# A chunked recurrence on a core of Trainium2: its small products spread over four 64x64 tiles of the matmul array, and a reordered stage ahead of it

## What is computed

```python
def wkv7_scan(r, decay, k, v, kk_neg, kk_b, reverse):
    def step(state, inp):
        r_t, w_t, k_t, v_t, an_t, b_t = inp
        sa = jnp.einsum('bhij,bhj->bhi', state, an_t)
        state = (state * w_t[:, :, None, :] + sa[..., None] * b_t[:, :, None, :]
                 + v_t[..., None] * k_t[:, :, None, :])
        return state, jnp.einsum('bhij,bhj->bhi', state, r_t)
...
rwkv_feat = centred_shift(proj[..., :RWKV_COLS], shift_taps)
...
for direction, reverse in ((0, False), (1, True)):
    ...
    y = y + wkv7_scan(heads(r), heads(decay), heads(k_dir), heads(v), -kk, kk * heads(a), reverse)
```

## Time and profile before

| | us |
|---|---|
| median of 3 runs (5455.51 to 5463.51) | 5456.74 |
| the profiled execution, whole | 5460.31 |
| its span, first to last instruction | 5458.5 |
| `rwkv_inputs` | about 1385 to 2060 of the span |
| `recurrence` | 2062 to 3275 |
| TensorE busy, of the span | 4692.6 (86%) |

### The profile page before, as it was taken

The page is one execution under the profiler, slowest core; times in us unless marked ns, Lnnn a source line. Parts: engine busy times, 40 slices in busy tenths (PEclk is TensorE's granted clock), DMA queues, the critical chain, the costliest instruction groups (busy, mean ns, idle before and its releaser), DMA issues. The chain is left out here.

```text
span 5458.5 us, 141686 instructions
## 1 busy us (share of the span) xinstructions
PE 4692.6 (86%) x60038; PEld 4316.4 (79%) x60038; DVE 3104.5 (57%) x6054; ACT 2090.0 (38%) x4040; POOL 1089.2 (20%) x829
## 2 busy tenths in 40 slices
PE   6878888886788877999999997881299999999998
PEld 5757666664677776999999995661199999999998
DVE  6867777775677774444444444556644444444443
ACT  3347777774455551111111111220044343434343
POOL 4432222221233332000000212210010101010100
PEclk9989999998899998999999998995599999999999
DMA  7810000000433322212122114430155555555553
GB/s 156 155 45 15 14 12 16 12 12 25 153 124 124 123 100 93 61 50 62 50 62 61 50 53 148 148 129 5 41 168 159 170 159 170 166 164 167 163 160 111
DMA packets 496709, 526.44 MB, mean 96 GB/s; under 512 B 74224, under 2 KB 434672, under 8 KB 496240
## 3 DMA queue, kind: packets, MB, share of 16 engines
q1 hardware_dynamic: 390256, 413.95, 23.8%
q10 hardware_dynamic: 92480, 62.93, 5.0%
q0 software_dynamic: 13504, 42.30, 3.5%
HBM read 372.12 MB, written 146.99 MB: 95 GB/s over the span
## 5 line engine op out<-in xcount | busy, mean ns | idle before, releaser
L2185 DVE TENSOR_TENSOR g_wlo<-g_raw,g_whi 128x2048 fp32r<-128x2048 f32 x192 | 439.1, 2287 | 129.6 <-ACT g_whi L2147 129.6
L615 PE MATMUL sapS<-KT,saq 128*128 128x512 f32 x1024 | 369.3, 443 | 123.0 <-ACT saprob L515 115.1
L2147 ACT ACTIVATE g_whi<-g_raw 128x2048 fp32r<-128x2048 f32 x192 | 365.8, 1905 | 246.3 <-DMA g_raw<-expert_w_gate 246.3
L568 DVE TENSOR_REDUCE samx<-sapS 128x1 f32<-128x512 f32 x512 | 352.5, 689 | 184.1 <-PE sapS L615 178.6
L2252 PE MATMUL g_pD<-g_whi,g_hh 128*128 128x256 f32 (+1 forms) x1536 | 437.4, 285 | 0.6
L2252 PE MATMUL g_pD<-g_whi,g_hl 128*128 128x256 f32 (+1 forms) x1536 | 429.4, 280 | 0.0
L2252 PE MATMUL g_pD<-g_wlo,g_hh 128*128 128x256 f32 (+1 forms) x1536 | 429.3, 279 | 0.0
L1426 DVE TENSOR_TENSOR d_zy<-d_zy,d_pZ 128x128 f32<-128x128 f32 x720 | 178.0, 284 | 416.2 <-PE d_pZ L1465 416.0
L523 ACT ACTIVATE saph<-sapT 128x512 fp32r<-128x512 f32 x512 | 305.8, 598 | 225.6 <-PE sapT L630 219.2
L505 POOL TENSOR_SCALAR saprob<-saprob,sarden 128x2048 f32<-128x2048 f32 x128 | 254.8, 1990 | 654.5 <-DVE sarden L587 654.5
L1115 PE MATMUL c_pP<-c_xh,c_whi 128*128 128x258 f32 x1120 | 343.2, 306 | 43.1 <-DMA c_gup<-g_lora_up 27.8
(11 more groups left out here) (383 smaller groups left out, 13246.1 us busy)
## 6 DMA issues: line engine op xcount, KB each, us to landing
g_raw<-expert_w_gate SPq DMA_DIRECT2D x64, 1024.0 KB, 5.3
g_raw<-expert_w_up SPq DMA_DIRECT2D x64, 1024.0 KB, 5.4
g_raw<-expert_w_down SPq DMA_DIRECT2D x64, 1024.0 KB, 5.2
ops<-c_ops SPq DMA_DIRECT2D x40, 1024.0 KB, 4.0
d_bd<-ops SPq DMA_DIRECT2D x80, 512.0 KB, 4.2
c_xh<-xT_hi SPq DMA_DIRECT2D x10, 1032.0 KB, 6.3
c_xl<-xT_lo SPq DMA_DIRECT2D x10, 1032.0 KB, 8.6
x_in<-x SPq DMA_DIRECT2D x20, 512.0 KB, 7.9
```

What stands on the lines that cost most here:

```text
L568: ins = dve.tensor_reduce(mx[:, h % 2, k:k + 1], pS[k][:], AX.X, ALU.max)
L615: mm = pe.matmul(pS[k][:], q[:, h // GH, h % GH, :], KT[:, 2 * (h // GH) + p, key0 + k * 512:key0 + (k + 1) * 512], start=(p == 0), stop=( ...
L2147: act.activation(w_hi[:, Q % NBUF, :, :], raw[:, Q % NRAW, :, :], ACT.Copy).then_inc(s["g_hi"], 1)
L2185: dve.tensor_tensor(w_lo[:, Q % NBUF, :, :], raw[:, Q % NRAW, :, :], w_hi[:, Q % NBUF, :, :].bitcast(F32), ALU.subtract).then_inc(s["g_lo" ...
```

## The change

In **`recurrence`**:

- Some products are written across: head h's product goes to the other half of the partitions (`heads(True, ...)`), that is, to the array's two other tiles (rows 0 to 63 with columns 64 to 127, and the reverse). Crossed are `between`, Z, `through`, `solved` and a new product x4 (below). x1, x2, x3, Y, `values`, `turned`, `state` and `out` stay straight.
- In the code a crossed and a straight product alternate, pair of heads by pair of heads: x1 with `through`, x3 with x4, the first half of x2 with `solved`, its second half with level 0's P, Z with Y. From level 1 on P is issued with the first calls of the block that it shares (`state`, `values`, `out`, `turned`); the rest of the block follows, straight alone. The order of the blocks changes: `values` is now before `turned`.
- x4 is added (16 calls a turn): d_zy's second half is computed by its own product into pZ, and no longer masked from d_br. Y goes to the upper half of pP's bank, since pZ now holds Z or x4. Semaphores d_Z and d_Y take the place of d_ZY.
- DVE's `begin` finishes direction 0 (d_br, then d_zy) before direction 1. The state update of direction 0 stands between the two masks of level 1, that of direction 1 after level 1's sums. ACT's copies follow the new order.

In **`rwkv_inputs`**: DVE does both `decays` at the start of a slot and moves `shift(n, 0)` ahead of the keys; ACT does `exps(q, 1)` ahead of `mid(n, 1)`; in even slots `bonus(q)` goes behind `tile(n, 5)` and `norms(n)` on TensorE.

```diff
@@ rwkv_inputs, ACT
                 mid(n, 0)
+                exps(q, 1)
                 mid(n, 1)
-                exps(q, 1)
@@ rwkv_inputs, DVE
                 decays(q, 0)
+                decays(q, 1)
+                shift(n, 0)
                 keys_b(q, 0)
                 keys_a(q, 0)
                 keys_c(q, 0)
-                shift(n, 0)
-                decays(q, 1)
+                if n % 2 == 0:
+                    shift(n, 1)
                 keys_b(q, 1)
-                shift(n, 1)
                 keys_a(q, 1)
                 keys_c(q, 1)
+                if n % 2:
+                    shift(n, 1)
@@ rwkv_inputs, PE
                     tile(n, 4)
-                    bonus(q)
                     tile(n, 5)
                     norms(n)
+                    bonus(q)
@@ recurrence, DVE
-                    dve.tensor_tensor(zy[par][g][:, :, 1, :], br[par][g][:, :, 0, :], bc(beside[:, 1 - g, 0:1, :], [P, RT, C]), ALU.mult).then_inc(s["d_in"], 1)
+                    dve.wait_ge(s["d_x4"], 2 * m + g + 1)
...
+                    dve.tensor_tensor(zy[par][g][:, :, 1, :], slim(pZ[g]), bc(beside[:, 1 - g, 0:1, :], [P, RT, C]), ALU.mult).then_inc(s["d_in"], 1)
...
                 for l in range(NL):
-                    between(n + 1, 1 - par, l)
+                    for g in range(2):
+                        between(n + 1, l, g)
+                        if l == 1 and g == 0:
+                            state(n, par, 0)
+                    for g in range(2):
+                        grown(n + 1, 1 - par, l, g)
                     if l == 1:
-                        state(n, par)
-                    grown(n + 1, 1 - par, l)
+                        state(n, par, 1)
@@ recurrence, PE
+            def heads(cross, out, l, r, first=True, last=True):
+                for h in range(2):
+                    mm = pe.matmul(out(halves[1 - h if cross else h]), l(halves[h]), r(halves[h]), start=first, stop=last)
+                return mm
...
+                for j in range(RT):
+                    mm = x1(par, g, j)
+                    if n is not None:
+                        through(1 - par, g, 2 * j)
+                        side = through(1 - par, g, 2 * j + 1)
...
+                can_x3(m, g)
+                for j in range(RT):
+                    mm = x3(par, g, j)
+                    side = x4(par, g, j)
...
+            def keys(m, par, g, n=None):
+                pe.wait_ge(s["d_br"], 2 * m + g + 1)
+                if n is not None:
+                    can_solve(n, g)
+                for j in range(RT // 2):
+                    x2(par, g, j)
+                    if n is not None:
+                        solved(1 - par, g, 2 * j)
+                        side = solved(1 - par, g, 2 * j + 1)
...
+                can_between(m, 0, g)
+                for j in range(RT // 2):
+                    mm = x2(par, g, RT // 2 + j)
+                    between(par, g, 0, 2 * j)
+                    side = between(par, g, 0, 2 * j + 1)
...
+            def grown(m, par, l, g):
+                pe.wait_ge(s["d_Pe"], 2 * (NL * m + l) + g + 1)
+                for j in range(RT):
+                    if l < NL - 1:
+                        side = grown_z(par, g, l, j)
+                    mm = grown_y(par, g, l, j)
...
+            def state_and_between(n, m, par, g):
+                pe.wait_ge(s["d_uc"], 2 * n + g + 1)
+                can_between(m, 1, g)
+                for j in range(RT):
+                    state(1 - par, g, j)
+                    side = between(par, g, 1, j)
+                side.then_inc(s["d_P"], 1)
+                for i in range(RT, 2 * RT):
+                    mm = state(1 - par, g, i)
+                mm.then_inc(s["d_sn"], 1)
```

More of the change, by code:

```diff
@@ L1335, in keys @@
                 for g in range(2):
[L1336 to L1339 removed]
+                    if more:
+                        values(n + 1, 1 - par, g)
                 for g in range(2):
[L1341 to L1342 removed]
@@ L1344, in values @@
-            def values(m, par):
+                    out(n, par, i, g)
                 for g in range(2):
[L1346 to L1370, removed]
+                    if more:
+                        turned(n + 1, 1 - par, g)
@@ L1371, in _ @@
+            for g in range(2):
+                keys(0, 0, g)
+            for g in range(2):
+                values(0, 0, g)
+            for g in range(2):
+                turned(0, 0, g)
             with act.Fori(0, NCH // 2 - 1) as i:
@@ L1452, in _ @@
             turn(NCH - 2, 0)
-            state(NCH - 1, 1)
+            for g in range(2):
+                state(NCH - 1, 1, g)
         @block.tensor
@@ L1458, in _ @@
             pe.wait_ge(s["d_dm"], 1)
-            def products(out, *terms):
-                for j in range(RT):
-                    for k, (l, r) in enumerate(terms):
-                        for h in halves:
-                            mm = pe.matmul(out(h, j), l(h, j), r(h, j), start=(k == 0), stop=(k == len(terms) - 1))
-                return mm
-            of = lambda m, x=None: (lambda h, j: m[h, j, :]) if x is None else (lambda h, j: m[h, j, x, :])
-            into = lambda m: lambda h, j: slim(m)[h, j, :]
@@ new lines, in turned_and_between, with between_alone @@
+            def turned_and_between(m, par, g):
+                pe.wait_ge(s["d_vc"], 2 * m + g + 1)
+                can_between(m, 4, g)
+                for j in range(RT):
+                    turned(par, g, j)
+                    side = between(par, g, 4, j)
+                side.then_inc(s["d_P"], 1)
+                for i in range(RT, 2 * RT):
+                    mm = turned(par, g, i)
+                mm.then_inc(s["d_bk"], 1)
+            def between_alone(m, par, l, g):
+                can_between(m, l, g)
+                for j in range(RT):
+                    mm = between(par, g, l, j)
+                mm.then_inc(s["d_P"], 1)
@@ L1517, in through @@
[L1517 to L1525 removed]
+                    grown(m, par, 1, g)
@@ L1562, in _ @@
-            begin(0, 0, 0)
-            keys(0, 0)
-            turned(0, 0)
-            values(0, 0)
-            for l in range(NL):
-                between(0, 0, l)
-                grown(0, 0, l)
-            for n in range(NCH - 1):
-                turn(n, n % 2, n // 2)
-            through(NCH - 1, 1)
-            solved(NCH - 1, 1)
-            state(NCH - 1, 1)
-            out(NCH - 1, 1)
+                    turned_and_between(m, par, g)
+                for g in range(2):
+                    grown(m, par, 4, g)
@@ L1577 @@
+            for g in range(2):
+                pe.wait_ge(s["d_tmp"], 2 * n + g + 1)
+                for i in range(3 * RT):
+                    mm = out(par, g, i)
+                mm.then_inc(s["d_yo"], 1)
 NE = 16
```

316 lines of the change are left out of this document (205 added, 111 removed).

## The result

The changed kernel takes **5403.8 us** (median of 4 runs, 5401 to 5417), the kernel before 5457.1; the ratio is 0.9905, with a 95% interval of 0.9887 to 0.9923. It is faster, as forecast, by 53 us and not by 443. The range on record, 4900 to 5305, doesn't hold it.

The account below looks back on a forecast made before the run. It took the recurrence to be bound by TensorE's two tiles, with stalls and a lower clock in `rwkv_inputs`. 5460.3 - 333 (recurrence) - 110 (`rwkv_inputs`) = 5017 us profiled, 5014 as median; range 4900 to 5305.

Parts of the forecast that it names:

- What bounds before: two tiles at 0.0295 us a record: Recurrence before: TensorE's 896 records a turn on two tiles, 0.0295 us each, in a turn of 29.55 us.
- Four tiles side by side: Recurrence: straight and crossed tiles work together though they share rows; four starts within 0.06 us in level 1.
- Rivals 1 and 2: Recurrence: starts limited as a whole (5301 us, 19%), or tiles that share rows disturb each other (6112 us, 6%).
- Rival 1: Recurrence: four tiles together get no more than 0.0295 us a record; 28.4 us a turn, 5301 us in all; 19%.
- "I take 0.4" for "issue": Recurrence, near the turn's end: added TensorE waits for instructions, 0.4 us a turn, between nothing and 1.2.
- The sum of 21.0 us: Recurrence: forecast length of a new turn, from 19.9 us over its levels plus additions of 0.7 and 0.4.
- The chain, 19.9 us: Recurrence: begin and levels 0 to 4 summed along TensorE's blocks and DVE's masks and sums, 19.9 us a turn.
- L1407 beside POOL's masking, 0.7 us: Recurrence: direction 1's L1407 slowed by coinciding with POOL's masking of d_kr, 0.7 us a turn, up to 0.95.
- Rival 3: Recurrence: the clock falls to its lower level, starts nearly twice as far apart; 33.1 us a turn, 5485 us; 3%.
- `rwkv_inputs`, 11.3 us a pair: Saving per pair of slots from shorter stalls, clock and earlier `c_wag`; 11.3 us, about 110 in all, bounds 38 and 133.
- `norms`: 2 less forecast: `rwkv_inputs`, odd slots: TensorE's 4.1 us wait at `norms` shrinks by 2 us; bounds 1.3 more and 4.1 less.
- The 1.5 for the earlier `c_wag`: `rwkv_inputs`, even slots: shifting `c_wag` earlier frees a bank earlier, saving 1.5 us a pair of slots.

Follow-up runs that it names:

- small_load: The changed kernel with operand loads from the third chunk on cut to two of 32 KB per direction, computing on old operands: 5350.3 us, ratio 0.9799.
- shift1: The changed kernel with `shift(n, 1)` put back ahead of `keys_b(q, 1)` in odd slots of `rwkv_inputs`: 5395.9 us, ratio 0.9879.
- bonus_only: The kernel before, with only `bonus` in even slots of `rwkv_inputs` issued after tile 5 and `norms`: 5408.5 us, ratio 0.9909.
- flip0: The changed kernel with products by the identity (`values`, `turned`) of the first row half written as one-pass transposes: 5589.0 us, ratio 1.0236.

## Why the prediction was wrong

- **What bounds before: two tiles at 0.0295 us a record.** Right, and what hid the other limit. 128 records of 32 or 64 columns, one page, take 128 x 0.0295 = 3.78 us on two tiles; a page is there after 3.81 (small_load). Both limits stood at nearly the same height, and only one could be seen. Before, a page came each 4.25 us, and the instruction queue stood in the profile; the prediction didn't read it.
- **Four tiles side by side.** Right: four starts within 0.02 us at the same place as forecast. Rivals 1 and 2 are wrong as mechanisms. Rival 1's size is nearly right (28.4 us a turn, measured 29.4): a limit on starts as a whole exists, as an average over pages, not between single starts.
- **"I take 0.4" for "issue".** This is the step that failed. The prediction saw 48.8 us of "issue", read it as an effect of the load, and bounded it at 1.2 us a turn by doubling it. 27.9 of the 48.8 are one wait at the stage's start, and the rest counts loads and matmuls; TensorE's matmuls had 0.25 us a turn. It is 6.5 now. A wait that is small since consumption is just slow enough doesn't double when consumption goes up by a third; it takes most of the gain. The sum of 21.0 us should have been held against 7.3 pages, 7.3 x 3.8 = 28 us.
- **The chain, 19.9 us.** Not tested fully. Turns of 25.2 us still follow the pages. 29.4 less 6.5 are 22.9 us, an upper bound; part of them is at the lower clock.
- **L1407 beside POOL's masking, 0.7 us.** Wrong, with little weight: its 68 records from 2113.6 to 3083.3 took 691 to 693 ns (it is L1412 now). VectorE busy 13 us a turn: right (524.39 / 40 = 13.1).
- **Clock.** Rival 3's sign came true (0.90 in the recurrence, 1.00 before), but not as the cause: the stall of 1.20 us at 2562.29 ends a stretch at 1.00, and 219 us of stalls are left at 0.95 in `small_load`. Its 33.1 us a turn did not come. In the windows above a page took 4.1 us at 0.58, almost without a stall, and 3.6 to 3.8 at 1.00 with one.
- **`rwkv_inputs`, 11.3 us a pair.** Measured 3.6. `bonus` stalls: 3.8 forecast, 36.1 us in nine waits measured, 4.0 each, right. `norms`: 2 less forecast, 1.4 more measured (41.9 to 55.7 in ten). That is the second failed step: the 1.3 us of longer queue on VectorE was taken to be absorbed by idle time. `shift1`, with less ahead of `shift(n, 1)`, has 6.7 us there, so what stands ahead of that shift sets the wait. Clock: 4 forecast; bonus_only saves 5.7 a pair, 3.3 of it stalls, so at most 2.4 are left for the clock (0.92 to 0.95). The 1.5 for the earlier `c_wag` became a wait for `c_k` of 18.6 us where 15.3 were.

## What to carry to other kernels

Before giving a saturated TensorE more tiles, count its instructions: a product of f32 on a 64x64 tile is four here, and in this stage 256 instructions took no less than 3.8 us on average, 0.030 us for a load with its matmul. When the new pace asked for more than that, the gain stopped there, and fewer instructions or calmer DMA traffic helped. And where a change consists of several moves in one stage, try each alone; one of them (one line, 49 us) was worth nearly as much as the whole (53).

## What the runs showed of the hardware

- Instructions come to TensorE in pages of 256 by a DMA of 16 KB each. The mean distance was 3.81 us with little other traffic (`small_load`) and 4.02 with the loads (after); a packet itself takes 1.0 us.
- Tiles that share rows of the array load and multiply side by side: 0.058 us a record each, four starts in 0.02 us. The Trainium skill has in "TensorE: Matmul & The Clock Gate", Part 3, that a load overlaps matmuls in flight only where the row group differs; these rows speak against it.
- In `flip0` no tile starts a product in the 0.14 us before a transpose that follows matmuls, nor in the 0.17 us behind it.
- At the lower clock level a tile's starts are 0.10 to 0.11 us apart, also with all four tiles at work, and 0.058 at the full one. A window at the lower level and the timeline of PE in it (after):

```profile
2533.90:2535.40 1.50, 1.43 (x56) 1.44 (x56) 0.49 (x2) 0.00 (x0) 0.00 (x0) 0.50 0.06 11
```
```profile
2534.10 0.30 PE L1474 MATMUL d_pZ<-d_pm,d_zy 64*64 64x32 f32 x2
...
2534.20 0.30 PE L1474 MATMUL d_pZ<-d_pm,d_zy 64*64 64x32 f32 x2
...
2534.31 0.30 PE L1474 MATMUL d_pZ<-d_pm,d_zy 64*64 64x32 f32 x2
```
